# Expert weights in one load a chunk, and a gather between two splits, in a hybrid attention and mixture-of-experts layer

## The reference, cut to what matters

```
for e in range(N_EXPERTS):
    he = jax.nn.silu(t @ w1[e]) * (t @ w3[e])
    y = y + gates[:, e:e + 1] * (he @ w2[e]).astype(jnp.float32)
```

## Time and profile before

| | us |
|---|---|
| median of three runs | 1198.0 (1196.94 to 1200.09) |
| profiled execution, own time | 1200.9 |
| its span, first to last instruction | 1199.0 |
| TensorE busy | 1067.9 (89%) |
| VectorE busy | 697.8 (58%) |
| ScalarE busy | 524.5 (44%) |
| GpSimd busy | 343.2 (29%) |
| TensorE's granted clock, mean over the span | 0.959 |

### The profile page before, as it was taken

One profiled execution on the slowest core, in us unless ns is written; L12 is line 12 of the kernel. 1 busy time (PEld: TensorE's weight loads), 2 busy tenths in 40 slices (PEclk: granted clock), 3 DMA queues, 4 the chain that ended last, 5 costly groups with the idle time before them and its releaser, 6 DMA issues.

```text
span 1199.0 us, 18236 instructions
## 1 busy us (share of the span) xinstructions
PE 1067.9 (89%) x5777; PEld 862.4 (72%) x5777; DVE 697.8 (58%) x1326; ACT 524.5 (44%) x1025; POOL 343.2 (29%) x368
## 2 busy tenths in 40 slices
PE   5999999999988899999999999975899999999950
PEld 4889889985555677777778787863777787877840
DVE  4330610117766667576565655448767777777867
ACT  4432421213532333323333333313777787888823
POOL 3100510000541111111110101102665565656755
PEclk9999999999888899999999999986999999999985
DMA  8340141122579586565555444825988787877677
GB/s 279 110 163 1 45 142 48 50 83 57 198 273 357 197 303 242 192 232 214 208 198 199 156 171 143 305 117 166 323 294 301 247 281 244 287 245 255 257 239 275
DMA packets 105764, 242.83 MB, mean 203 GB/s; under 512 B 15248, under 2 KB 63840, under 8 KB 95456
## 3 DMA queue, kind: packets, MB, share of 16 engines
q1 hardware_dynamic: 81312, 117.42, 28.9%
q0 software_dynamic: 23328, 122.17, 28.7%
q10 hardware_dynamic: 1056, 2.36, 0.6%
HBM read 243.31 MB, written 48.94 MB: 244 GB/s over the span
## 4 chain that ended last, share of the span: by engine, by line
PE 58%; DMA 13%; DVE 9%; issue 7%; SPq 5%; ACT 5%; POOL 2%; POOLq 0%; ACTq 0%; DVEq 0%
DMA below<-in_w 8%; PE ps L1078 4%; PE ps L2196 4%; PE ps L2197 4%; PE ps L2198 4%; PE ps L931 4%; PE ps L949 3%; SPq L1428 3%; PE ps L1119 3%; PE ps L1027 3%; PE ps L1120 3%; PE ps L2191 3%; PE ps L2190 3%; PE ps L2192 3%; PE ps L1123 3%
## 5 line engine op out<-in xcount | busy, mean ns | idle before, releaser
L1846 DVE TENSOR_TENSOR low<-below,high 128x1024 fp32r<-128x1024 f32 x128 | 157.0, 1260 | 36.6 <-ACT high L1543 36.2
L1642 PE MATMUL ps<-high 128*128 128x512 f32 x384 | 155.7, 406 | 11.2 <-DVE low L1856 7.4
L1518 POOL TENSOR_TENSOR low<-below,high 128x1024 fp32r<-128x1024 f32 x62 | 127.9, 2064 | 95.7 <-ACT high L1563 94.7
L1644 PE MATMUL ps<-high,low 128*128 128x512 f32 x384 | 150.8, 393 | 0.0
L1643 PE MATMUL ps<-low,high 128*128 128x512 f32 x384 | 150.6, 392 | 0.0
L1543 ACT ACTIVATE high<-below 128x1024 fp32r<-128x1024 f32 x128 | 130.4, 1069 | 41.5 <-DMA below<-in_w 41.3
L655 ACT ACTIVATE arena<-ps 128x512 f32<-128x512 f32 (+8 forms) x100 | 50.1, 510 | 170.6 <-PE ps L931 170.2
L931 PE MATMUL ps<-arena 128*128 128x128 f32 (+4 forms) x613 | 93.3, 274 | 7.8 <-ACT arena L655 2.2
L799 POOL DMA_DIRECT2D high<-wo_dram x34 | 18.6, 548 | 280.1 <-PE ps L1123 269.2
L1642 PEld LDWEIGHTS ps<-high 128*128 128x128 f32 x384 | 72.6, 189 | 28.3 <-issue 11.6
L949 PE MATMUL ps<-arena 128*128 128x64 f32 (+2 forms) x624 | 82.9, 268 | 6.9 <-DVE arena L704 2.9
(11 more groups left out here) (251 smaller groups left out, 2224.7 us busy)
## 6 DMA issues: line engine op xcount, KB each, us to landing
below<-in_w SPq DMA_DIRECT2D x256, 256.0 KB
high<-wo_dram POOLq DMA_DIRECT2D x36, 1024.0 KB, 6.0
low<-wo_dram POOLq DMA_DIRECT2D x36, 1024.0 KB, 8.4
below<-in_w POOLq DMA_DIRECT2D x64, 512.0 KB
y_dram<-arena SPq DMA_DIRECT2D x32, 512.0 KB, 5.7
arena<-in_x_prompt SPq DMA_DIRECT2D x15, 512.0 KB
below<-in_w_in SPq DMA_DIRECT2D x14, 512.0 KB, 7.7
out<-arena SPq DMA_DIRECT2D x9, 512.0 KB, 2.7
```

The source lines that it names most:

```text
L1518: pool.tensor_tensor(w2_lo[s % UN][:, c], w2_in[:, c], w2_hi[s % UN][:, c].bitcast(F32), ALU.subtract).then_inc(s_w2lo, 1)
L1642: pe.matmul(out, x_hi, w_hi, start=start, stop=False)
L1644: return pe.matmul(out, x_lo, w_hi, start=False, stop=stop)
L1846: dve.tensor_tensor(chunk(w13_lo[j], c), chunk(w13_in, c), chunk(w13_hi[j], c).bitcast(F32), ALU.subtract).then_inc(s_w13lo, 1)
```

## The change

The host puts `w1` and `w3` side by side into one array `w13` (1024 x 512 an expert), so that one row of a chunk is 2 KB long in DRAM where it was 1 KB in each of two arrays. SyncE issues one DMA of 512 KB a chunk where it issued two of 256 KB, and the semaphore of a chunk counts 16 a slot instead of 32. On GpSimd the gather for the slot two ahead moves from ahead of the first split of a slot to between its first and second split.

```diff
@@ moe_loads @@
-            rows13 = [w[0, bass.ds(e, 1)].rearrange("e (c p) f -> p (e c) f", p=P) for w in (w1, w3)]
+            rows13 = w13[0, bass.ds(e, 1)].rearrange("e (c p) f -> p (e c) f", p=P)
             for c in range(WC):
...
                     sp.wait_ge(s_w13lo, split)
-                for k in range(2):
-                    sp.dma_start(w13_in[:, 2 * c:2 * c + 2, k * FF:(k + 1) * FF], rows13[k][:, 2 * c:2 * c + 2, :],
-                                 cond=new).then_inc(s_w13in[c], 16)
+                sp.dma_start(w13_in[:, 2 * c:2 * c + 2, :], rows13[:, 2 * c:2 * c + 2, :],
+                             cond=new).then_inc(s_w13in[c], 16)
@@ moe_pool @@
-            if s + UN < SLOT_TILES:
-                gather(s + UN)
             if s == SLOT_TILES - 2:
                 fetch_first(range(SOON))
             if s + 1 < SLOT_TILES:
                 for c in range(2):
+                    if c and s + UN < SLOT_TILES:
+                        gather(s + UN)
                     pool.wait_ge(s_w2hi, 2 * s + c + 1)
                     pool.tensor_tensor(w2_lo[s % UN][:, c], w2_in[:, c], w2_hi[s % UN][:, c].bitcast(F32),
                                        ALU.subtract).then_inc(s_w2lo, 1)
@@ moe_act, split_weights @@
-                act.wait_ge(s_w13in[c], 32 * (s + 1))
+                act.wait_ge(s_w13in[c], 16 * (s + 1))
@@ moe_dve, split_weights @@
-                dve.wait_ge(s_w13in[c], 32 * (s + 1))
+                dve.wait_ge(s_w13in[c], 16 * (s + 1))
@@ kernel @@
+    inputs["w13"] = np.concatenate([inputs["w1"], inputs["w3"]], axis=-1)
```

More of the change, by code:

```diff
@@ L104, in hybrid_layer @@
                  kv_norm, w_uq, w_uk, w_uv, hg_lb_logits, hg_gnorm, w_o, ffn_norm, w_router_group, b_router_group,
-                 w_router_expert, b_router_expert, w1, w3, w2, final_norm, table, level_masks,
+                 w_router_expert, b_router_expert, w13, w2, final_norm, table, level_masks,
                  y_prompt, y_sample, ckv_prompt, krope_prompt, hgrn_prompt, ckv_sample, krope_sample, hgrn_sample):
@@ L2282 @@
         "kv_norm", "w_uq", "w_uk", "w_uv", "hg_lb_logits", "hg_gnorm", "w_o", "ffn_norm", "w_router_group",
-        "b_router_group", "w_router_expert", "b_router_expert", "w1", "w3", "w2", "final_norm"]
+        "b_router_group", "w_router_expert", "b_router_expert", "w13", "w2", "final_norm"]
 _OUTS = [(1, 1024, D), (1, SAMPLE, D), (1, 1, 1024 + META, CR), (1, 1, 1024 + META, RD), (1, 1, HH, HK, HK),
@@ L2295 @@
     arrays, args = {}, []
+    inputs["w13"] = np.concatenate([inputs["w1"], inputs["w3"]], axis=-1)
     for name, a in [(n, np.ascontiguousarray(inputs[n])) for n in _INS] + [("table", table), ("masks", level_masks)]:
-        if name in ("w1", "w2", "w3"):
+        if name in ("w13", "w2"):
             a = np.ascontiguousarray(a.reshape(1, NG, EG, *a.shape[2:]).swapaxes(1, 2).reshape(a.shape))
```

## The result

The changed kernel takes 1227.5 us (median of 4 runs, 1224.0 to 1231.0) against 1197.9 for the one before: 1.0232 times as long, 95% interval 1.0204 to 1.0260. The forecast was 1208, with 1219 as the upper end of its range. The direction was right, the size a third of what came: 29.6 us instead of 10.

The account below looks back on a forecast made before the run. Waits for gate/up and down weights in the expert loop were taken as the bound. Pairs +5, early slots +4.4 and tail +1 made +10.4 us on 1200.9, so 1211.3, or 1208 against the median; eight-in-ten range 1190 to 1219.

Parts of the forecast that it names:

- the pairs: Ten pairs of slots, 913.4 to 1111.4 us, a new expert then the same one; forecast +0.5 each, +5 us.
- early stretch: Six slots from 848.5 to 913.4 us, where new experts follow each other; forecast 4 x 1.1 = +4.4 us.
- Step 1: Gate/up loads: one transfer of 2 KB pieces per chunk gains 0.12 us a chunk, about 0.5 us an expert.
- Step 2: SyncE: four DMA issues instead of eight are hidden behind full DMA engines, so worth zero.
- Step 3: GpSimd: the gather between the splits makes each second-slot down-weight load 1.6 us later, bounds zero to 2.3 us.
- give-back of 1.1 us: In each pair, the gate/up stall of 10.43 - 9.30 = 1.1 us goes, as that load gets more time.
- Step 4: Later gathers against TensorE's transposes: just hidden in the middle stretch, 0 to 3 us in the tail, taken as +1.
- Rival (d): Middle stretch: transposes wait for late gathers too, 10 us more than before plus the early 4.4, 1213 us; chance 0.04.
- (a): Down-weight loads have room and only gate/up loads count, so the change gains: -10.5, 1188 us; chance 0.26.
- (b): Gains and losses cancel, a pair +0.2 or less and the early slots sharing the gain: 1198 us; chance 0.18.
- (c): Down weights lose DMA share to 2 KB pieces, +0.65 on 14 loads, 9 us over the forecast, 1217 us; chance 0.12.
- (e): The merged gate/up transfer is no faster at all, 4 x 0.5 more, 1210 us; counted within the forecast's 0.40.

Follow-up runs that it names:

- e1: The changed kernel with the gather back at its old place ahead of the first split, so the merged gate/up transfers alone: 1196.9 us.
- e12: e1 with three register reads ahead of the down-weight loads, which makes them 2.25 us later: 1218.3 us.
- e8: e1 with an extra GpSimd operation on 352 columns (1.1 us) between the splits, gather at its old place: 1214.8 us.
- e3: The changed kernel with the gather issued ahead of the first split but behind the wait for ScalarE, some 2 us sooner: 1215.3 us.
- e10: e1 with gate/up weights loaded for the first slot only: 1182.8 us.
- e11: The changed kernel, gather moved, with gate/up weights loaded for the first slot only: 1209.9 us.

## Why the prediction was wrong

**Bounds and stages (right).** The loss lies in the loop of the slots, most of it in the pairs: +18.3 us where I had +5. The early stretch grew by 0.4 where I had +4.4: between e1 and the changed kernel the move costs 5.2 us there, against 4 x 1.6 forecast, and the merge gives 4.8 back instead of 2. The tail cost 3.8 where I had 1. The floor of 9.3 stands, and slots that wait for nothing still take it.

**Step 1, the merged transfer (rate right, gain too large, no harm).** The gate/up queue alone in the changed kernel, from 975.2 to 977.7 us and from 1062 to 1066 us:

```profile
DMA packets 522, 1.01 MB, mean 402 GB/s; under 512 B 31, under 2 KB 31, under 8 KB 522
...
q1 hardware_dynamic: 522, 1.01, 105.0%
...
DMA packets 624, 1.20 MB, mean 300 GB/s; under 512 B 38, under 2 KB 38, under 8 KB 624
...
q1 hardware_dynamic: 624, 1.20, 93.3%
```

The second stretch is not full (93.3%). In 2.5 us stretches of the pairs that are full (over 100%) and hold nothing else, pieces of 2 KB move at 330 to 402 GB/s, median 376, and the 1 KB pieces of before at 344 to 356, median 351. So the 388 that I had taken from another stage is near what came, and the 356 was right. What failed is the 0.5 us an expert: from SyncE's first issue to the end of the split of the last chunk e1 needs 0.15 us less than before without the first pair and 0.3 with it. Where the rest of the 0.5 went isn't shown. By stage: 0.6 us for the pairs where I had 5, and 4.8 early where I had 2. The sum, 2 us in e1's median against my 7, is among the smaller errors.

**Step 2, fewer issues at zero.** Nothing contradicts it: e1 bounds merge and issues together.

**Step 3, the delayed down load (delay right, consequences half).** The load is issued 7.0 us after the high part instead of 5.3, 1.7 later against 1.6 forecast. That such a delay lengthens "to new" holds: 1.95 us in e12 for 2.25. Two things failed. The first is the place from which I started: I read 9.93 for "to new" from the one interval at 1072, but its mean over the pairs is 9.40, and 10.40 stands for the other. The pair that I read so took 20.36 us and the mean pair 19.8, and I added the 0.5 of the one to the other; with "to new" at 11.2 the sum of 20.3 left 9.1 for "from new", less than the floor. The second is that nothing was charged for moving the second split itself. e8 has the gather's length at the gather's place and no gather, and its "from new" grows by 0.87 instead of shrinking by 1.1. In the changed kernel that collision is mild (first low split 1.50 us, against 1.42 in e1), as everything on GpSimd comes still later there. The splits of the new expert's own chunks do get longer, the first to 2.0 us from 1.3 and the last to 1.6 from 1.2; whether that is on the path wasn't tested.

The prediction also named a sign: it is wrong if the down-weight wait doesn't grow. It forecast over 30 us in the middle stretch, and the wait is 18.7 there, as before (over the span it grew from 26.1 to 33.1). What hides it is the late gather, by which ScalarE comes to the down weights later: where the gather is sooner, in e3, the wait is 31.9.

**The give-back of 1.1 us (came, and was taken).** ScalarE's gate/up wait in the pairs fell from 19.0 to 9.8 us, as forecast under 10. Yet "from new" went from 10.40 to 10.22 only. Of its ten intervals, four have 3.41 us each at a granted clock of half (1.2 of 2.4 GHz), and none had in the kernel before: they take 10.92 to 10.98, while the other six are 9.74 in the mean, four of them between 9.32 and 9.81. The windows around one (columns as above, clock third from the end):

```profile
1045.40:1047.80 2.40, 0.01 (x1) 0.00 (x0) 2.40 (x2) 1.10 (x2) 1.49 (x1) 1.00 0.25 99
...
1048.80:1052.20 3.40, 3.40 (x11) 2.66 (x10) 2.19 (x4) 2.03 (x3) 2.65 (x2) 0.50 0.29 110
```

TensorE stands still for 2.4 us, waiting for the gather, and then runs 3.41 us at the low clock: products start every 0.43 us that start every 0.23 at the full one. So a wait of 2.4 us cost about 4. Not every wait does this: the nine before first slots last 1.1 to 2.5 us, and the low clock followed four of the five that lasted 2.0 or more. Nor does it take a late gather: e8 and e12 have two such stretches each in the middle. Four times 1.6 is 6.4 us, 0.64 a pair, which agrees with the 5.8 by which TensorE's busy time grew. With the low clock taken off, the give-back is 0.8 of the 1.1.

**Step 4, the late gather (the step that failed).** The prediction called it "just hidden" in the middle, with a landing at 1053.1 against a need at 1053.3, because I took the median of all 32 gathers, 6.6 us. Those of "to new" slots share the engines with a gate/up load; in the kernel before they took 6.7 to 8.3 us, 7.7 in the mean, and the others 5.4. The median is a figure between two groups, of which only the slow one matters. With 7.7 the landing would have been 1054.2, 0.9 after the need even with step 3's delay. Rival (d) was this mechanism, at a chance of 0.04 and 1 us a pair over the old time. In the profile after, nine gathers of ten for the slots that end a "to new" interval have landed 0.2 to 0.3 us before their transposes, where they had 3.1 to spare; "to new" is 11.41, or 11.65 without the last, where no expert is new. Against the 11.2 forecast that is only 0.2 to 0.5, but it lies on the path and brings the low clock with it. In the tail the gather took 9.6 us from issue to landing beside the residual loads, above the longest of before (9.1), and the interval to slot 29 is 12.9 instead of 9.3: 3.6 where I had taken 1 from a range of 0 to 3.

**Sum over a pair.** Forecast 20.3, measured 21.6. The low clock is 0.64 of the gap, "to new" 0.2, and the rest, 0.5, lies in "from new", which stays at 9.6 without the low clock where the forecast of the pair left 9.1. What that rest is stays open. In experiments: e3, where gathers are 2 us sooner and the down load nearly as late (6.4 against 7.0), stands 1.1% below the changed kernel; I read that as the price of the late gather, low clock included. It isn't clean: VectorE's first low split takes 2.56 us in e3, against 1.50 in the changed kernel, so e3 has e8's collision and the gather may cost more. e8 stands 1.4% above e1; that is the price of the later split and load. The two together are the 2.5% between the changed kernel and e1, but that they fit is partly luck: each works through another mixture of waits than the two together, as the longer down-weight wait and the collisions in e3 and e8 show. How e8's 17 us divide between the later load and the collision stays open: by e12's 20 us for 2.25, a load 1.05 later would be some 9 of them, if it went in proportion, which wasn't shown.

**The other rivals.** (a) had a point that I passed over: in the kernel before only the "from new" intervals were long, and e10 shows that they are the gate/up loads' alone. But the merge did not shorten them. (b) is out, as the time rose clear of noise. (c) predicted down loads that take longer beside 2 KB pieces; e1 has both, its down-weight wait in the pairs is 18.4 against 18.9 and its time isn't above that of before, so it is out as well. (e), a merged transfer that is no faster, is nearer to e1 than my 0.5 us an expert in the pairs, but not in the early stretch.

## What to carry to other kernels

When a transfer is issued later, take its landing time from those instances that meet the same traffic, not from the median of its line, and count the wait ahead of its new place too: here the slack was 3 us, the place in the program moved by one split and the issue by more than 5 us (1040.9 to 1046.5 in the prediction's own rows), and the transfer then closed a ring of its own. Two operations back to back in front of a load are not a free slot for a third one: 1.1 us there cost 17, because a later operation on GpSimd delays the load and meets VectorE's where they had missed each other. Price a new wait of TensorE above its length: of five that lasted 2.0 to 2.5 us here, four were followed by 3.4 us at half the clock.

## What the hardware showed that I had not expected

A gather can stand behind the other queue's backlog before its first packet. The one issued at 1061.86 has its first packets near 1066.5, after the gate/up queue has moved 1.2 MB in the four microseconds before (the second half of the fence under step 1 lists no other queue), and lands at 1070.35. The nine gathers of the pairs that meet the gate/up load in the changed kernel have their first packets 1.2 to 3.7 us after their issue ends; the others, and all of e11's in the pairs, where there is no such load, 0.7 or 0.8. At its old place the gather landed 8.5 us after issue in e1's first slots against 7.7 before, and slack hid it.

A low split on VectorE lasts 1.2 us alone. In the run of four below, from the changed kernel, the first takes 2.4 us beside GpSimd's split from 1041.13 to 1043.16, and the last, which starts at 1046.44 beside GpSimd's split from 1046.31 to 1048.38, takes 3.0:

```profile
1041.81 7.65 DVE L1845 TENSOR_TENSOR low<-below,high 128x1024 fp32r<-128x1024 f32 x4 [0.52 <-ACT high L1542]
```
